# Who subtracts the lower parts: VectorE takes over the block factors of the up projection, and u of group 1 is subtracted at another place

## The reference, cut to what matters

```python
    x = x + gate1 * (merged @ w_out)
    h2 = _rmsnorm(x, norm2_g) * (1.0 + scale2) + shift2
    x = x + gate2 * (jnp.square(jax.nn.relu(h2 @ w_up)) @ w_down)
    ...
    y_sample = _rmsnorm(y_s, final_g)
```

## Time and profile before

| | us |
|---|---|
| median of 3 runs | 2749.95 |
| lowest and highest run | 2743.67, 2750.27 |
| the profiled execution | 2747.24 |
| its span, first to last instruction | 2745.5 |
| TensorE busy | 2587.4 |
| VectorE busy | 1485.9 |
| ScalarE busy | 964.4 |
| GpSimd busy | 863.0 |

### The profile page before, as it was taken

The page is one execution under the profiler, slowest core; times in us unless marked ns, Lnnn a source line. Parts: engine busy times, 40 slices in busy tenths (PEclk is TensorE's granted clock), DMA queues, the critical chain, the costliest instruction groups (busy, mean ns, idle before and its releaser), DMA issues. The chain is left out here.

```text
span 2745.5 us, 38037 instructions
## 1 busy us (share of the span) xinstructions
PE 2587.4 (94%) x15236; PEld 2282.5 (83%) x15236; DVE 1485.9 (54%) x2071; ACT 964.4 (35%) x1633; POOL 863.0 (31%) x478
## 2 busy tenths in 40 slices
PE   6779999899999999999999899988999998999998
PEld 3568888788888898888787688977999996888886
DVE  8768765365555445444886511587444443343336
ACT  5352221155555545454311611353333331211112
POOL 2459982001110110100344223364333343332220
PEclk9999999999999999999999999988999998999999
DMA  8787765512313231311877322531232245222202
GB/s 279 250 272 228 237 219 195 191 55 94 116 40 116 103 106 40 116 70 50 310 234 258 141 92 77 195 127 64 95 104 98 91 159 230 75 77 77 77 31 77
DMA packets 130629, 375.16 MB, mean 137 GB/s; under 512 B 14485, under 2 KB 50423, under 8 KB 130070
## 3 DMA queue, kind: packets, MB, share of 16 engines
q1 hardware_dynamic: 110486, 302.47, 31.5%
q0 software_dynamic: 19968, 70.26, 7.7%
HBM read 267.30 MB, written 96.99 MB: 133 GB/s over the span
## 5 line engine op out<-in xcount | busy, mean ns | idle before, releaser
L88 PE MATMUL tl_b<-tl_uhi,tl_whi 128*128 128x512 f32 (+1 forms) x768 | 275.3, 358 | 13.5 <-DVE tl_x L3241 11.2
L89 PE MATMUL tl_b<-tl_ulo,tl_whi 128*128 128x512 f32 (+1 forms) x768 | 274.0, 357 | 0.0
L90 PE MATMUL tl_b<-tl_uhi,tl_wlo 128*128 128x512 f32 (+1 forms) x768 | 273.3, 356 | 0.0
L88 PE MATMUL at_out<-h_hi,hd_nexthi 128*128 128x424 f32 (+1 forms) x672 | 264.6, 394 | 6.8 <-PEq L80 3.5
L3241 DVE SCALAR_TENSOR_TENSOR tl_x<-tl_b,all_mod,tl_x 128x512 f32<-128x512 f32 (+1 forms) x192 | 125.5, 660 | 252.4 <-PE tl_b L90 251.9
L547 POOL TENSOR_TENSOR hd_nextlo<-at_raw,hd_nexthi 128x1024 fp32r<-128x1024 f32 x26 | 61.4, 2360 | 629.2 <-ACT hd_nexthi L647 629.2
L729 DVE TENSOR_REDUCE at_nmax<-at_s 128x1 f32<-128x1280 f32 (+1 forms) x160 | 196.8, 1272 | 104.3 <-PE at_s L598 103.6
L2910 POOL TENSOR_TENSOR tl_wlo<-tl_raw,tl_whi 128x1024 fp32r<-128x1024 f32 x54 | 132.0, 2445 | 354.5 <-ACT tl_whi L2689 290.4
L89 PE MATMUL at_out<-h_lo,hd_nexthi 128*128 128x424 f32 (+1 forms) x672 | 239.7, 357 | 0.0
L90 PE MATMUL at_out<-h_hi,hd_nextlo 128*128 128x424 f32 (+1 forms) x672 | 239.5, 356 | 0.0
L682 ACT ACTIVATE at_e<-at_s,at_nmax 128x1280 f32<-128x1280 f32 (+1 forms) x160 | 185.3, 1159 | 135.6 <-DVE at_nmax L729 135.6
(11 more groups left out here) (459 smaller groups left out, 7022.4 us busy)
## 6 DMA issues: line engine op xcount, KB each, us to landing
tl_raw<-in_w_tail SPq DMA_DIRECT2D x87, 512.0 KB, 3.4
hy_tab<-in_hy_tab POOLq DMA_DIRECT2D x68, 512.0 KB, 5.9
tl_ur<-s_u SPq DMA_DIRECT2D x32, 640.0 KB, 7.5
hd_wa<-in_w_adaT SPq DMA_DIRECT2D x32, 512.0 KB, 4.4
at_raw<-in_w_proj SPq DMA_DIRECT2D x26, 512.0 KB
s_u<-tl_x SPq DMA_DIRECT2D x32, 384.0 KB, 2.8
s_gatesT<-at_pad SPq DMA_DIRECT2D x16, 640.0 KB, 2.9
mg_gate<-s_gatesT SPq DMA_DIRECT2D x16, 640.0 KB, 5.1
```

The source lines that it names most:

```text
L88: pe.matmul(out, w_hi, x_hi, start=first, stop=False, skip_group_check=loose)
L89: pe.matmul(out, w_hi, x_lo, start=False, stop=False, skip_group_check=loose)
L90: return pe.matmul(out, w_lo, x_hi, start=False, stop=last, skip_group_check=loose)
```

## The change

VectorE makes all lower parts of the late factors (b22, t1, t2, t3, t4 of both parts); GpSimd's `late_lower` is gone, and GpSimd goes from the first pair's weights straight to the second's. The places of `tokens`, `late_lower`, `weight_sums`, `square`, `out_weights`, `sum_up` and `empty` in the lists of VectorE and ScalarE are new, so that square sum n of quad 2 follows the add of n+1, and the add of x = 31 stands ahead of the weight sums. `EMPTIED` takes (0,1,1) and (0,2,1) ahead of (1,1,0) and (1,2,0). VectorE's `lower_u(1)` moves from down add 2 to down add 15; that of later groups stays at 2. SP loads the third and fourth down weight (w+2, w+3) at the last pair's job 3, before and after the first four rows of x1; they stood behind all rows of x1, and behind u of group 1. GpSimd subtracts w+1 before u of group 0 instead of after it. No operation is added or dropped.

```diff
--- before.py
+++ after.py
@@ -2404,7 +2404,8 @@
     rest = [(q, i, g) for q in range(1, PAIRS_UP) for i in (1, 2, 5, 6, 3, 7, 4) for g in range(2)]
     rest = [x for x in rest if x not in early]
     last = [(PAIRS_UP - 1, i, g) for i in (1, 2, 5, 3, 6, 7, 4) for g in range(2)]
-    parts = [(0, i, 0) for i in (1, 2, 5, 6, 3, 7, 4)] + early + [(0, i, 1) for i in (1, 2, 5, 6, 3, 7, 4)]
+    parts = [(0, i, 0) for i in (1, 2, 5, 6, 3, 7, 4)] + [(0, i, 1) for i in (1, 2)] + early
+    parts += [(0, i, 1) for i in (5, 6, 3, 7, 4)]
     return begun + first + early + second + rest[:-len(last)] + last, parts + rest
 
 
@@ -2631,8 +2632,10 @@
             for job in UPS:
                 q, i, p = job
                 if (q, i, p) == (PAIRS_UP - 1, 3, 0):
+                    load(N_OUT + 2 * PAIRS_UP + 2)
                     sp.wait_ge(up_mm, UP_AT[PAIRS_UP - 1, 3, 1] + 1)
                     load_rows(range(HK))
+                    load(N_OUT + 2 * PAIRS_UP + 3)
                 if i in (3, 4):
                     store_u(job)
                 if (i, p) == (2, 1):
@@ -2645,11 +2648,11 @@
                 elif job == (PAIRS_UP - 1, 7, 1):
                     sp.wait_ge(up_mm, UP_AT[PAIRS_UP - 1, 7, 1] + 1)
                     load_rows(range(HK, KD))
-                    load(N_OUT + 2 * PAIRS_UP + 2)
             first = N_OUT + 2 * PAIRS_UP
             load_u(1)
             for j in range(3, N_DOWN):
-                load(first + j)
+                if j > 3:
+                    load(first + j)
                 if j % GT == 3 and j // GT + 2 < GROUPS:
                     load_u(j // GT + 2)
             for j, c in enumerate(C_ORDER):
@@ -2830,14 +2833,13 @@
             out_weights(KD + W_SLOTS + 3)
             for h in range(2):
                 first_upper(1, h)
-            square(SQ0)
-            square(SQ0 + 1)
-            out_weights(2 * KD)
-            square(SQ0 + 2)
-            for n in range(3, KD):
+            for n in range(4):
                 square(SQ0 + n)
-                if n < 6:
-                    out_weights(2 * KD + n - 2)
+            for n in range(4, KD):
+                if n < KD - 1:
+                    out_weights(KD + W_SLOTS + n)
+                square(SQ0 + n)
+            out_weights(KD + W_SLOTS + KD - 1)
             for j in range(4):
                 out_weights(2 * KD + W_SLOTS + j)
                 if j == 0:
@@ -2854,27 +2856,28 @@
             square(2 * KD + 5)
             late_upper("t3", 0)
             square(2 * KD + 6)
+            square(2 * KD + 7)
             up_weights(0, 1)
-            late_upper("t4", 0)
-            square(2 * KD + 7)
+            empty((0, 1, 0))
             up_weights(0, 2)
             up_weights(0, 3)
             deviation(3, at[3])
-            empty((0, 1, 0))
+            empty((0, 5, 0))
+            late_upper("t4", 0)
             for k in range(KD):
                 shift(3, k)
-                if k == 4:
-                    empty((0, 5, 0))
-            empty((0, 6, 0))
+                if k == 3:
+                    empty((0, 6, 0))
             late_upper("b22", 1)
             prepare((0, 5, 0))
             late_upper("t1", 1)
             late_upper("t2", 1)
             empty((0, 4, 0))
             late_upper("t3", 1)
+            empty((0, 1, 1))
             empty((1, 1, 0))
             late_upper("t4", 1)
-            for job in EMPTIED[9:]:
+            for job in EMPTIED[11:]:
                 empty(job)
                 prepare(job)
                 if job == (PAIRS_UP - 1, 5, 1):
@@ -2921,16 +2924,6 @@
                     src = sums_w[:, 2 * i - 2:2 * i]
                 pool.tensor_tensor(g_lo[i][:], src, g_hi[i][:], ALU.subtract).then_inc(gl_done, 1)
 
-            def late_lower(name, p, at):
-
-                hi, lo, src = f[name, p]
-                if name == "b22":
-                    src = x1[:, HK:KD, quad(PARTS_OF[p][1])]
-                elif name == "t1":
-                    pool.wait_ge(t_made, 4 * p + 2)
-                pool.wait_ge(late_h, 5 * p + at)
-                pool.tensor_tensor(lo, src, hi, ALU.subtract).then_inc(low[name], 1)
-
             def lower_u(group):
 
                 s = group % 2
@@ -2948,25 +2941,18 @@
 
             for j in range(1, N_OUT):
                 weights(j)
-            late_lower("b22", 0, 1)
-            up_weights(0, 0)
-            late_lower("t1", 0, 2)
-            up_weights(0, 1)
-            late_lower("t3", 0, 4)
-            up_weights(0, 2)
-            up_weights(0, 3)
+            for i in range(4):
+                up_weights(0, i)
             up_weights(1, 0)
-            late_lower("b22", 1, 1)
-            late_lower("t1", 1, 2)
-            late_lower("t3", 1, 4)
             for i in (1, 2, 3):
                 up_weights(1, i)
             for q in range(2, PAIRS_UP):
                 for i in range(4):
                     up_weights(q, i)
             weights(N_OUT)
+            weights(N_OUT + 1)
             lower_u(0)
-            for j in range(N_OUT + 1, N_OUT + 4):
+            for j in range(N_OUT + 2, N_OUT + 4):
                 weights(j)
             lower_u(1)
             for j in range(4, N_DOWN + GT):
@@ -3172,10 +3158,12 @@
                 dve.wait_ge(first_h, 2 * p + h + 1)
                 dve.tensor_tensor(lo, x1[:, HK * h:HK * h + HK, quad(p)], hi, ALU.subtract).then_inc(first_l, 1)
 
-            def late_lower(name, p, at):
+            def late_lower(name, p):
 
                 hi, lo, src = f[name, p]
-                dve.wait_ge(late_h, 5 * p + at)
+                if name == "b22":
+                    src = x1[:, HK:KD, quad(PARTS_OF[p][1])]
+                dve.wait_ge(late_h, 5 * p + ("b22", "t1", "t2", "t3", "t4").index(name) + 1)
                 dve.tensor_tensor(lo, src, hi, ALU.subtract).then_inc(low[name], 1)
 
             def weight_sums(q):
@@ -3300,11 +3288,12 @@
             sum_up(SQ0 + 1)
             for h in range(2):
                 first_lower(1, h)
+            sum_up(SQ0 + 2)
+            sum_up(SQ0 + 3)
             for n in range(5, KD):
                 out_add(2 * KD + n)
-                sum_up(SQ0 + n - 3)
-            for q in range(2 * KD - 3, 2 * KD):
-                sum_up(q)
+                sum_up(SQ0 + n - 1)
+            sum_up(SQ0 + KD - 1)
             out_add(3 * KD)
             scale_of(2, quad_tiles(2))
             for n in (1, 2):
@@ -3321,31 +3310,39 @@
             tokens("t3", 0)
             out_add(3 * KD + 5)
             sum_up(2 * KD + 4)
+            late_lower("t1", 0)
             tokens("t4", 0)
-            weight_sums(0)
             out_add(3 * KD + 6)
             sum_up(2 * KD + 5)
-            late_lower("t2", 0, 3)
+            out_add(3 * KD + 7)
+            weight_sums(0)
+            late_lower("t2", 0)
             sum_up(2 * KD + 6)
-            late_lower("t4", 0, 5)
-            out_add(3 * KD + 7)
             sum_up(2 * KD + 7)
             scale_of(3, quad_tiles(3))
+            late_lower("b22", 0)
+            late_lower("t3", 0)
             for k in range(KD):
                 modulate(3, k)
                 if k == 3:
                     empty((0, 2, 0))
+                    late_lower("t4", 0)
+                elif k == 5:
+                    empty((0, 3, 0))
+                    empty((0, 7, 0))
             tokens("t1", 1)
             tokens("t2", 1)
+            late_lower("t1", 1)
             tokens("t3", 1)
-            empty((0, 3, 0))
-            empty((0, 7, 0))
             tokens("t4", 1)
-            late_lower("t2", 1, 3)
-            late_lower("t4", 1, 5)
+            late_lower("t2", 1)
+            empty((0, 2, 1))
+            late_lower("b22", 1)
+            late_lower("t3", 1)
+            late_lower("t4", 1)
             empty((1, 2, 0))
             weight_sums(1)
-            for job in EMPTIED[9:]:
+            for job in EMPTIED[11:]:
                 empty(job)
                 if job[1:] == (2, 1) and job[0]:
                     weight_sums(job[0] + 1)
@@ -3356,7 +3353,7 @@
             for x in range(len(DOWNS)):
                 j, n, c = DOWNS[x]
                 if x < FIRST_LAST:
-                    if x % (NC * KD) == 2 and j // GT + 1 < GROUPS:
+                    if x % (NC * KD) == (2 if x >= NC * KD else 15) and j // GT + 1 < GROUPS:
                         lower_u(j // GT + 1)
                     down_add(x)
             for x in range(FIRST_LAST, len(DOWNS)):
```

## The result

| | before | after |
|---|---|---|
| median of the runs | 2749.17 (4 runs) | 2729.56 (4 runs) |
| lowest and highest run | 2743.67, 2750.27 | 2727.84, 2735.18 |
| the profiled execution, its span | 2747.24, 2745.5 | 2735.18, 2733.4 |

The change took 19.6 us off by the medians, where 20.5 were forecast (2729). The ratio of the runs' times, after to before, is 0.9936 with a 95% interval of 0.9917 to 0.9956, that is 12 to 23 us.

A forecast was written before the change was run, and what follows sets the result against it. TensorE, 94% busy, was bound where it waited on a late VectorE, held by SBUF turns with GpSimd or its own queue order. Gains of 5.5 + 15.0 = 20.5 us gave 2729; range 2718 to 2741.

The forecast's parts named there:

- Square sums of quad 2 at 1815.9, then 3 us for the spread: Before the block products: last sum at 1815.9 instead of 1819.0, then TensorE waits some 3 us for the spread.
- First product at 1846.0, no wait before the second: Start of the block products: first at 1846.0 instead of 1854.76, and the 5.62 us wait for the second gone.
- Token sums of quad 3 at 1857.5 with a wait of 5: After (0,1,1): 1857.5 instead of 1867.25, new wait about 5 us; sign: VectorE's 1536 subtractions at 1.75 us except t2 low.
- (1,1,0) at 1879.9 after 4 us: Pair 1's start, behind a chain through three in-order queues: 1879.9 after a new 4 us TensorE wait.
- (1,1,1) at 1897 to 1898.5: Start of the steady state: 1897 to 1898.5 against 1903.45, with 1 to 3 us before mixing (0,7,1).
- Part 2: Handover to the down projection, u of the second group, loads and w+1: gain 15.0 us (12 to 16).
- Loads and w+1: 0 to +1.6, 0.9 taken: Handover: two new 1.2 us waits replace the 2.27 us wait and its 1.6 us of clock; 0.9 us gained.
- B: Rival, SBUF lock not in turns or meetings fall well: early sums, token sums about 1852.5; 2724 to 2719; chance 0.2.
- C: Rival, part 1 gives nothing: t4's upper part and last two modulations hold pair 1; 2735, or 2737; chance 0.12.
- part 1: Lower parts moved from GpSimd to VectorE with new list orders, up to (1,1,1): gain 5.5 us (1 to 12).
- D: Rival at the handover: the u wait moves to down product 24, same 11 us; gain 5.5 to 6.5, 2744; chance 0.08.
- E: Rival, clock: new short waits keep TensorE at 1.2 GHz from 1846 to 1898, 26 us more; 2755; chance 0.05.

The follow-up runs named there:

- part 1 only: After with every line of part 2 (lower_u(1) move, early loads, w+1 order) as it was in before; 2746.25 us against 2749.91, ratio 0.9986.
- the moved line alone: Before with one edit, VectorE's lower_u(1) moved from down add 2 to 15; 2733.03 us, ratio 0.9943.
- new order, old engines: After with lower parts of b22, t1 and t3 given back to GpSimd in their old places; 2737.96 us, ratio 0.9965.
- the 2x2 table: Four kernels, all with part 2, b22, t1, t3 on GpSimd or VectorE: old order 0.9937, 0.9918; new order 0.9965, 0.9936 (again 0.9927).
- all three: After with quad 3's last square sums before weight sums, (1,1,0)'s chain reordered, quad 2's deviation before ScalarE's weight half; 2723.26 us, ratio 0.9914.
- part 2 only: Before with lower_u(1) moved, w+2 and w+3 loaded early, w+1 subtracted before u of group 0; 2732.04 us, ratio 0.9937.
- rest of part 2 only: Before with early loads of w+2 and w+3 and GpSimd's w+1 first, lower_u(1) not moved; 2743.49 us, ratio 0.9975.

## Why the prediction held, point by point

The forecast of 2729 met 2729.56. Times of after less 9.1 stand against the forecast's.

- *Square sums of quad 2 at 1815.9, then 3 us for the spread.* 1825.21 less 9.1 is 1816.1, with 1.08 us of wait left; the spread waited 2.97. Right.
- *First product at 1846.0, no wait before the second.* 1855.05 less 9.1 is 1845.95, and no wait. Right, and by the stated way: t3 and t4 at 1.75, one sum held back (2.23 us).
- *Token sums of quad 3 at 1857.5 with a wait of 5.* 1855.9, after 4.62: 1.6 us early. I had put three of GpSimd's parts in between, and had t2's lower part held up. It went through in 1.75 us, ahead of the first of them, against what I had named as a sign. Two sums then met two of the parts (1858.18, x2); the third, 1.28 us in the earlier trace rows, was asked for at 1864.60, behind the second sum. The term held one turn too many.
- *(1,1,0) at 1879.9 after 4 us.* 1877.6 after 3.95. VectorE stood 2.53 us for t4's upper part, as said. The chain behind it was the stated one: ScalarE's b22 upper part, ready at 1883.3, then the new pair's weight at 1884.2, then GpSimd's 2.35 us, which ended last. b22's upper part started 2.2 us sooner than said, which is where the early sums show.
- *(1,1,1) at 1897 to 1898.5.* 1895.7, with 2.44 us (1 to 3 said) before (4,1). Early by 1 to 3 us, given back by a cost I left out: behind the 2.44 us wait the clock falls, and (1,1,1) to H takes 363.75 instead of 361.3. The two errors nearly cancel, 5.3 for 5.5. That this is so close is luck: the same instructions gave 2.1 in part 1 only.
- *Part 2.* Two waits of 1.07 and 0.74 (two of 1.2 said), none at down product 6, u split from 2287.4, VectorE at it 41.0 us after H (2309.60 less 2268.58; 2306 less 2264.75 is 41.3), nothing at product 24. u is there earlier than said, 18.8 us after H instead of 23.8, which costs and gives nothing. 15.9 for 15.0: the 2.27 us with its clock are gone, as said, and the two new waits cost 1.8 instead of 2.4.
- *Loads and w+1: 0 to +1.6, 0.9 taken.* Beside the moved line 0 to 0.5 (464.9 without, 464.4 to 464.9 with), where 2.27 less 1.8 would be 0.5. The 1.6 of clock that I credited them for can't be seen there, for in the one profile of the moved line alone the clock happened not to fall. In before and in part 1 only it fell behind the same wait, and with the loads it fell in none of ten profiles. So the split of the 15.9 between the line (14.1 to 15.8) and the loads stays open by these 1.6 us; their sum does not.

**The rivals.** B (the lock not in turns, 2724 to 2719): its early sums came by 1.6 of 5 us; the 4.62 us wait stayed, and the earlier trace rows repeated in new order, old engines. It fell. C (part 1 gives nothing, 2735): part 1 gives 5 by the two profiles of after, and 3.7 by its own runs, with an interval from 0.8 to 6.9. Its mechanism was at work, and 3.5 of the 8.8 us won at the first product were eaten up behind it; not all. D (the wait moves to product 24): no wait there in any of the kernels with the moved line. It fell. E (clock): half clock behind the waits of 3.54, 4.62, 3.95 and 2.44 us, for about 3.4, 3.4, 6.2 and 5.9 us, of which I had not counted the last. In between the clock came back, and the mean from 1850 to 1905 was 0.86. It fell.

**What it did not see.** That the reordering, most of the diff, gives nothing that can be seen beside the engine. The sum followed the new order as a whole and never asked what the old one would do with GpSimd out of the way; the 2x2 table is what would have shown it.

**Turns.** The Trainium skill ("SBUF — State Buffer", Who interferes with whom) says that whoever starts first has the shared port pair for its whole instruction. The runs agree (in after a sum of 0.34 us, asked for at 1848.93 while GpSimd worked, took 2.23 and ended 0.3 us after GpSimd's part). The page says nothing of who comes next. Here an engine that waited went next, though the other had a queue (GpSimd with two parts queued let a sum of VectorE in between, 5.06 us for two sums of 0.34). Who asks first is not resolved below some 0.1 us: in after GpSimd's part stands at 1858.18 and VectorE's t2 lower part at 1858.19, and VectorE's went first.

## What to carry to other kernels

A subtraction on GpSimd is not free work beside a busy VectorE: here each one that met VectorE's cost it a turn of 1.8 to 3.3 us (0.34 to 2.18, 1.75 to 5.08). So when VectorE is on the path and the two work out of SBUF, ask first whether VectorE can take the work itself. An in-order engine's wait belongs after what others need from it; find the place where its input has long landed, and the transfer needs no hurrying (one line made 14 to 16 us here). And test a reordering apart from the change that comes with it: cut profiles at a mark ahead of the change, since the part before it moved by up to 10.6 us between the profiles here, and know how far two profiles of equal code differ behind that mark (3.3 us here).

## What the runs showed of the hardware that was not expected

- Operations of VectorE with one tensor from SBUF stand in the turns too. The prediction counted on it for quad 2's diagonal; its size for quad 3's was not expected: two diagonals, 0.48 us together where GpSimd is idle, took 4.08 in all three. ScalarE's are not held: 0.70 us for two beside GpSimd.
- A wait of 2.3 to 2.6 us drops the clock in one execution and not in another. The same wait of 2.27 us was followed by 0.50 in before and by 1.00 with the moved line alone; TensorE's wait before (0,7,1) was 2.60 us in before and 2.62 in part 2 only, the windows behind it 0.50 (1897.70 to 1900.60) and 1.00 (1902 to 1905). Of the four kernels that are equal up to there it fell in two (before, rest of part 2 only) and not in the other two. Such a fall cost 1.2 us there (3.5 us to the next job's start instead of 2.3), 1.6 by the estimate at the handover and 2.4 before H in after. How much of the spread between the runs of one kernel comes from this is not shown.
